# One 2 MB transfer for each expert weight matrix in place of two of 1 MB

## The reference

```python
combine = moe_route(flat, router_w, router_b)       # 2 of 16 experts for each token
for e in range(N_EXPERTS):
    hid = jax.nn.silu(flat @ w_gate[e]) * (flat @ w_up[e])
    out = out + combine[:, e:e + 1] * (hid @ w_down[e]).astype(jnp.float32)
```

## Time and profile before

| what | value |
|---|---|
| median of 3 runs (lowest to highest) | 1327.92 us (1326.81 to 1328.6) |
| the profiled execution, its time | 1327.52 us |
| its span | 1325.6 us |
| PE busy | 1097.7 us, 83% |
| DVE busy | 904.4 us, 68% |
| ACT busy | 565.1 us, 43% |
| bytes moved by DMA | 332.00 MB |

### The profile page before, as it was taken

How to read it: one execution, slowest core, us unless ns; L and a number is a source line. 1 busy time by engine, 2 the same in 40 slices (tenths; PEclk the granted TensorE clock), 3 DMA queues, 4 the chain that set the end, 5 groups by cost and what they waited for, 6 DMA issues and landing times. The chain is left out here.

```text
span 1325.6 us, 13246 instructions
## 1 busy us (share of the span) xinstructions
PE 1097.7 (83%) x4594; PEld 763.6 (58%) x4594; DVE 904.4 (68%) x1029; ACT 565.1 (43%) x558; POOL 174.0 (13%) x170
## 2 busy tenths in 40 slices
PE   6799999997777695469999999816638999999980
PEld 1344534445454542358888888716426888888870
DVE  0486775724566312749999999833674999999964
ACT  1511110011244301337777777501235777777741
POOL 0100210000100000041111110030023111111005
PEclk9799999998699898779999999967768999999995
DMA  8755685625000012279999999557227999999945
GB/s 339 253 211 204 254 317 208 221 79 206 0 1 0 0 63 55 81 232 390 412 413 413 414 413 414 237 191 293 94 96 237 405 414 414 414 413 413 412 164 222
DMA packets 141977, 332.00 MB, mean 250 GB/s; under 512 B 10480, under 2 KB 12472, under 8 KB 141808
## 3 DMA queue, kind: packets, MB, share of 16 engines
q1 hardware_dynamic: 127768, 288.60, 57.6%
q0 software_dynamic: 7488, 25.19, 4.9%
q10 hardware_dynamic: 6680, 17.67, 3.3%
HBM read 308.32 MB, written 23.15 MB: 250 GB/s over the span
## 5 line engine op out<-in xcount | busy, mean ns | idle before, releaser
L1421 DVE TENSOR_TENSOR w_lo<-ring,w_hi 128x2048 fp32r<-128x2048 f32 x192 | 428.1, 2283 | 28.3 <-ACT w_hi L1260 28.3
L1260 ACT CAST w_hi<-ring 128x2048 fp32r<-128x2048 f32 x192 | 362.6, 1909 | 74.3 <-PE bank L1538 49.0
L1538 PE MATMUL bank<-w_hi,xT_hi 128*128 128x512 f32 x512 | 205.8, 402 | 10.5 <-DVE xT_lo L1426 10.5
L1538 PE MATMUL bank<-w_lo,xT_hi 128*128 128x512 f32 x512 | 201.9, 394 | 0.0
L1538 PE MATMUL bank<-w_hi,xT_lo 128*128 128x512 f32 x512 | 201.9, 394 | 0.0
L1538 PEld LDWEIGHTS bank<-w_hi,xT_hi 128*128 128x128 f32 x512 | 97.8, 191 | 31.6 <-DVE xT_lo L1426 12.1
L922 PE MATMUL bank<-ring_last,arena 128*128 128x512 f32 x256 | 113.1, 597 | 0.0
L666 DVE SCALAR_TENSOR_TENSOR gate_b<-ring,silu_c,gate_b 128x512 f32<-128x512 f32 x140 | 107.4, 767 | 5.0
L922 PE MATMUL bank<-ring,arena 128*128 128x512 f32 (+1 forms) x256 | 109.2, 581 | 1.6 <-ACT arena L464 1.6
L1538 PEld LDWEIGHTS bank<-w_hi,xT_lo 128*128 128x128 f32 x512 | 97.8, 191 | 21.1
L1538 PEld LDWEIGHTS bank<-w_lo,xT_hi 128*128 128x128 f32 x512 | 98.0, 191 | 19.3
(11 more groups left out here) (217 smaller groups left out, 1231.8 us busy)
## 6 DMA issues: line engine op xcount, KB each, us to landing
ring<-in_moe_w_gate SPq DMA_DIRECT2D x64, 1024.0 KB, 8.7
ring<-in_moe_w_up SPq DMA_DIRECT2D x64, 1024.0 KB, 10.6
ring<-in_moe_w_down SPq DMA_DIRECT2D x64, 1024.0 KB, 9.0
ring<-in_ada_w SPq DMA_DIRECT2D x23, 2048.0 KB, 7.8
y_scratch<-arena ACTq DMA_DIRECT2D x32, 512.0 KB, 6.0
ring<-in_w_in SPq DMA_DIRECT2D x3, 2048.0 KB, 10.4
ring_last<-in_w_in SPq DMA_DIRECT2D x3, 2048.0 KB, 9.8
xh_scratch<-arena SPq DMA_DIRECT2D x8, 512.0 KB, 2.7
```

Source lines behind the costliest of these rows:

```text
L1260: nc.scalar.copy(w_hi[:, buf(u, p), :], half(raw(e, p))).then_inc(s_hi, 3 if isinstance(e, int) and (e, p) == (-1, 3) else 1)
L1421: V.tensor_tensor(w_lo[:, buf(u, p), :], half(raw(e, p)), w_hi[:, buf(u, p), :].bitcast(F32), ALU.subtract).then_inc(s_lo, 3 if isinstance ...
L1538: last = pe.matmul(bank[:, b, :], xs[:, kk, :], ws[:, k, :], start=(kk == 0 and i == 0), stop=(kk == KD - 1 and i == 2))
```

## The change

Each expert weight matrix is loaded by one transfer of 2 MB, with one semaphore, `matrix_load[q]`, for each of the three places. SP waits for the split of the second half of a place (p = 2q + 1) and then issues the load of the whole place. ACT waits for the whole matrix before it copies the first half of it. The splitting itself, its halves, and the orders on ACT, DVE and PE stay as they are.

```diff
-        half_load = [nc.alloc_semaphore(name=f"half_slot{r}_loaded") for r in range(6)]
+        matrix_load = [nc.alloc_semaphore(name=f"matrix_slot{q}_loaded") for q in range(3)]
...
-        def put_half(eng, l, e, r, into=None):
+        def put_matrix(eng, l, e, q, into=None):
-            into = r if into is None else into
-            w, rows, k = ((a["moe_w_gate"], D // 2, KD // 2), (a["moe_w_up"], D // 2, KD // 2),
-                          (a["moe_w_down"], DE // 2, KE // 2))[r // 2]
-            src = w[l][bass.ds(e, 1), (r % 2) * rows:(r % 2 + 1) * rows].rearrange("a (k p) c -> p (a k) c", p=P)
-            eng.dma_start(half(into).rearrange("p (k c) -> p k c", k=k), src).then_inc(half_load[into], 16)
+            into = q if into is None else into
+            w, k = ((a["moe_w_gate"], KD), (a["moe_w_up"], KD), (a["moe_w_down"], KE))[q]
+            src = w[l][bass.ds(e, 1)].rearrange("a (k p) c -> p (a k) c", p=P)
+            eng.dma_start(ring[:, into, :].rearrange("p (k c) -> p k c", k=k), src).then_inc(matrix_load[into], 16)
...
-                for h in range(4):
-                    put_half(sp, 0, 0, h)
+                for q in range(2):
+                    put_matrix(sp, 0, 0, q)
                 sp.wait_ge(m_op, NT)
-                for h in (4, 5):
-                    put_half(sp, 0, 0, h)
+                put_matrix(sp, 0, 0, 2)
...
-                    for p in range(4):
-                        sp.wait_ge(s_lo, pos_count(-1, p))
-                        put_half(sp, l, 1, p)
+                    for q in range(2):
+                        sp.wait_ge(s_lo, pos_count(-1, 2 * q + 1))
+                        put_matrix(sp, l, 1, q)
                     with sp.Fori(0, NE - 2) as i:
-                        for p in range(6):
-                            sp.wait_ge(s_lo, pos_count(i, p))
-                            put_half(sp, l, sp.snap(i + 2) if p < 4 else sp.snap(i + 1), p)
-                    for p in (4, 5):
-                        sp.wait_ge(s_lo, pos_count(NE - 2, p - 4))
-                        put_half(sp, l, LAST, p, raw(LAST, p))
+                        for q in range(3):
+                            sp.wait_ge(s_lo, pos_count(i, 2 * q + 1))
+                            put_matrix(sp, l, sp.snap(i + 2) if q < 2 else sp.snap(i + 1), q)
+                    sp.wait_ge(s_lo, pos_count(NE - 2, 1))
+                    put_matrix(sp, l, LAST, 2, 0)
...
-                        act.wait_ge(half_load[raw(e, p)], loaded(e, p))
+                        act.wait_ge(matrix_load[raw(e, p) // 2], loaded(e, p))
...
-                for r in range(6):
-                    put_half(sp, 1, 0, r)
+                for q in range(3):
+                    put_matrix(sp, 1, 0, q)
```

## The result

| | before | after |
|---|---|---|
| median (lowest to highest) | 1327.75 us (1326.81 to 1328.6) | 1354.9 us (1349.05 to 1356.24) |
| ratio, 95% interval | | 1.0188 (1.016 to 1.0215) |
| profiled execution, its span | 1325.6 us | 1354.3 us |
| expert loop of layer 0, PE's first to last product | 573.2 to 868.0: 294.8 us | 571.4 to 880.2: 308.8 us |
| expert loop of layer 1 | 998.9 to 1292.4: 293.5 us | 1008.8 to 1320.8: 312.0 us |

My forecast of 1328.2 us and its range up to 1333 were wrong. The two loops are 14.0 and 18.5 us longer; each starts about 2 us earlier than it would have, so that the profiled span grows by 28.7 us in all. Nothing outside the loops and their starts moved by more than a microsecond.

What follows compares the result with a forecast made beforehand. PE was taken to bound the loops at 17.65 us per expert, transfers close behind at 17.7. The terms 0 + 0 + 0 + 2 x 0.15 = +0.3 us on the 1327.92 median gave 1328.2 us, range 1325.5 to 1333.

Steps and rivals of the forecast that it cites:

- What bounds the kernel: Expert loops: PE sets the 17.65 us period, transfers close behind at 17.7; late issue loses nothing unless the queue runs dry.
- Part 1: SP in the loop: 96 instead of 192 issues, each about 0.37 us; saved and not visible, 0.
- Part 2: ACT's first-half copies wait for second halves; up 1.0 us late, at worst 1.8 of 4.2 us cover; cost to PE 0.
- Part 3: Loop loads start 2.2 to 3.9 us later; queue stays full by 0.5 us or more; cost 0, bounds 0 to 0.9 per expert.
- Part 4: Layer starts, first gather beside gate's load: bounds -0.5 to +1.3 us per layer, taken as +0.15.
- A: Rival, slower: one slot's circle, 17.3 or 18.5 us per expert, becomes the loop's period; 1331 to 1346 us; chance 0.16.
- B: Rival, about the same: contention at the two layer starts at its upper bound, +2.6 us, 1330.5 us; chance 0.10.
- C: Rival, faster: fewer, larger transfers relieve engines, only at the two layer starts; 1 us, or down to 1325; chance 0.05.
- My signs of being wrong: In the loop: PE gaps before products whose splits waited for a load, period above 17.8 us, or GB/s below 405.

Runs made afterwards that it cites:

- experiment 2: Kernel before, 1 MB loads issued as early as before, but ACT waits for both halves of a matrix before copying the first: 1327.8 us, ratio 0.9998.
- Experiments 1: Kernel before, both 1 MB halves issued only after the second half's split; ACT still copies each half when it is in: 1323.0 us, ratio 0.9951.
- experiment 6: Kernel before with 1 MB transfers, both issued after the second split, and ACT waiting for both halves: 1346.0 us, ratio 1.0121.
- experiment 4: Kernel before, but at each layer start the first half of expert 1's gate and up is issued with the second: 1322.9 us, ratio 0.9955.
- experiments 11: Kernel before with only down as one 2 MB transfer, its issue in the loop one split (2.2 us) later still: 1350.0 us, ratio 1.0167.
- experiment 7: Kernel before with only down as one 2 MB transfer (a layer's last down matrix stays in halves): 1327.9 us, ratio 0.9992.
- 3: Kernel before with gate and down each one 2 MB transfer, waited for whole; up in halves issued as before: 1356.9 us, ratio 1.0189.
- 10: Changed kernel with up's matrix as four 512 KB transfers issued together, ACT waiting for all: 1345.2 us, ratio 1.0107.
- 8: Kernel before with only gate as one 2 MB transfer, its first load of a layer late: 1348.9 us, ratio 1.0159.
- 5: Kernel before with only up as one 2 MB transfer; gate and down in halves, first load of a layer early: 1351.1 us, ratio 1.0162.

## Why the prediction was wrong
**What bounds the kernel: right.** PE with 17.65 us and the transfers with 17.7 us were the two candidates, and I wrote that a late issue is harmless only as long as the queue has not run dry. That was the whole question.

**Part 1 (issues): right**; no wait in the views above is put down to SP's issuing.

**Part 2 (ACT waits for the second half): right as far as it went.** I said that 1 to 2 us of lateness are absorbed before PE, and experiment 2 shows just that.

**Part 3 (issues later): the step that failed.** It put the cost of the late issue at 0: "The next up is issued at 702.98 [...], 3.8 us before gate has landed [...]. So the queue stays full by 0.5 us or more". Up's 3.8 us were nearly right; after the change it is 3.56 on average. It also took gate for the tightest place, with 3.0 us, and gave down 4.2; in the changed kernel gate has 5.0 and down 6.1, and up is the tightest. Above all, the size that they were compared with was wrong. I took 2.5 us for start and end, from one 2 MB load in an empty queue, and thought that any margin above it keeps the queue full. The runs show no loss at 5.0 us and above, and a loss at 4.1 us and below. In the changed kernel 1.15 us of transfer time go at the up shown above, and about as much at the others, where I had 0. I also wrote that when the loop falls behind, "this margin grows". It doesn't: up's issue is tied to its own landing by 6.6 us of copying and splitting, and the earlier transfers, down and gate, take 10.1 us (5.0 + 5.1), so the margin stays at 10.1 - 6.6 = 3.5 us however late everything is. Had I followed this circle once around for up, I would have seen a margin that nothing restores.

**Part 2 and Part 3 apart: the deeper error.** I priced the wait on the landing and the delay of the issue one by one, each with the other as it was. Experiments 1 and 2 show that each of them is free; experiment 6 shows that both together cost 1.2%. (Its gain at the start is in that number too, as in every one where the first loads are late.) Only together do they tie a whole landing to a whole issue.

**Part 4 (start of a layer): wrong sign.** I had -0.5 to +1.3 us for each layer and took +0.15. It gave back 2.5 us in each: PE's wait for the gathered rows, 9.30 in the earlier trace rows, is 6.82 after the change, and experiment 4 gets the same with nothing else changed. What this took away, a load beside the gather, I had priced at no more than 0.5 us. Before, the first load was issued 1.3 us behind the first gather and slowed it; now it is issued 3.5 us behind it.

**The rivals.** A was what came: the circle of one place as the period, and transfers and PE as full as each other. I described it on down, with 8.4 us from landing to split and 17.3 us in all, and it came on up, where the margin is the smallest. Its argument against, that a late landing shortens the time to its split, was true only in part (down's 8.4 us became 7.9, not 6.5) and no help. Its sum for the worst case, 17.3 + 1.3, is 18.6 and not 18.5. Its prices (0.3 to 0.9 us per expert) were too low: 0.9 and 1.2 us on average in the two layers of the changed kernel, and 1.3 in the middle of its loops. Over 14 steps in each layer that is 29 of the loops' 32.5 us. B fell by its sign. C's only true part is the start, 0.3 to 0.6% (experiment 4), which needs no larger transfer. My signs of being wrong (GB/s below 405, a period above 17.8 us, PE gaps before products whose splits waited) all came.

**Why 2.5 us were not enough.** The dip begins over 2 us before the earlier load has landed, and the semaphore records say why. Gate's 16 steps in the expert shown above come from 1130.2 to 1132.4. The first one is only 1.4 us behind the issue of up, and the rate falls from about 1130 on. I read each step as one of the 16 DMA engines that is through with its share and turns to the next load; the records don't number the engines. In experiments 11 and 7 one can see the new load start, since down's packets are of 4 KB and up's of 2 KB. In 11 down's first packet starts 1.4 us after its issue, and 24 of its packets up to the earlier landing take 229 to 768 ns where 159 is the rule. In 7 it starts 2.7 us after, and only one is slow. So the load is late for the shares that end first, though not for the landing.

The lead counts all 16 shares. Over 339 issues, those of the load with the smallest margin in each of the 14 kernels, the transfer time missing in the 7 us after the issue (against 413 GB/s) is 1.1 us on average at leads below 2.6 us, 0.7 at 2.6 to 3.0, 0.2 at 3.0 to 3.4 and 0.1 above. Single issues scatter widely around this, by up to 1 us and more, but every kernel with a mean lead of 3.5 us or more keeps its loops, and every one with 3.1 or less doesn't.

**What stays open.** The changed kernel loses more than experiment 6 at the same margin (3.56 and 3.60 us). Its lead is shorter, 2.6 us against 2.9, since the 16 steps of the load before up are spread over 1.8 us and not over 1.2. That goes with the greater loss, but no experiment changed the spread alone, and why it differs I don't know. Down at the same short lead loses less (11, 0.4 us an issue, against 1.0 for gate in 3), and I don't know why either. Four transfers of 512 KB are no better than two (10).

## What to carry to other kernels
With one place for each matrix, landing, copying out, issue and landing again make a circle; write it down for each place, and hold against it how long the other transfers keep the queue full from the landing on. The difference is the margin. The shares of the earlier load end over 1 to 2 us before it lands, so take that off, and if what is left is only a little above the start of a transfer, expect a loss. Price two edits on one circle together, since each may be free by itself. When PE and the transfers are equally full, keep transfers small enough to be issued early, and at a start keep big loads out of the way of a small one that is waited for.

## What the runs showed of the hardware
- To keep the rate, a load had to be issued well before the load ahead of it landed. With 5.0 us of margin the rate is 407 to 425 GB/s (experiment 7), with 3.1 us it is 336 in the 2 us before the earlier load's landing (11), and with 3.5 us 285 in the worst 2 us (after). A 2 MB load alone takes 7.6 us, 2.5 more than its bytes, and this did not tell the margin that is needed.
- The 16 steps of a load's semaphore came over 1.2 us (6) to 1.8 us (after) on average, and once over 5.9 us (8). On average, issues with a lead of 3.4 us or more lost 0.1 us of transfer time, and those with less than 2.6 us lost 1.1.
- Joining two transfers gave nothing in a full queue: the whole down takes 4.98 us from the landing before it to its own (7), its two halves 2.49 each before. The Trainium skill, page SBUF — State Buffer, section "The DMA setup-cost knee", would have one coalesce into the largest transfer, for a fixed cost of about 2 us each. The measurement decides here: with down joined the ratio is 0.9992 (7), and with all three joined, and so issued later and waited for whole, 1.0188.
- The first gather of a layer, 0.52 MB, landed after 8.0 to 8.5 us where the first load was issued 1.3 to 1.4 us behind it (before, 2, 5, 7, 11), and after 5.4 to 5.9 us where it was issued 3.5 to 3.6 us behind it (all others).
- In one stretch PE was idle for 4.4 of 6 us, and this was followed by a granted clock of 0.57 over the next 6 us (8). Gaps of 0.3 to 0.8 us did not move the clock from 1.00 (after, the two stretches shown).
